# A mixed transformer kernel on one core: the second block's input projections as seven block products instead of eight, with the depthwise convolution cut into pieces between their sums

## The chip, the core and the metric

The kernel runs on one core of a Trainium2 chip. The metric is device microseconds (us) of one execution. Beside each run of a changed kernel the kernel before is run on the same chip. All data are float32; each matmul of the program appears in the trace as two instructions, each with its own weight load.

## The reference, cut to what matters

A first block (a mixer and a feed-forward part) hands a 512-token sequence of width 1024 to a second block of two layers. At the head of each layer a normalised input is projected to 2048 columns, and a depthwise convolution of 31 taps, followed by a layer norm and a SiLU, runs on 256 channels of the result:

```python
u = h @ w_in_l                                  # 1024 -> 2048 columns
q_a, k_a = apply_axial_rope(...), apply_axial_rope(...)   # 512 and 128 columns
v_a, q_b, k_b, v_b = ...                        # 128, 256, 256, 256 columns
o_c = conformer_conv(u[..., OFF_C:], ...)       # 2 x 256 columns

def conformer_conv(u, conv_w, conv_b, ln_g, ln_b):
    a, gate = jnp.split(u, 2, axis=-1)
    h = a * jax.nn.sigmoid(gate)
    h = lax.conv_general_dilated(h, conv_w, ...) + conv_b   # 31 taps, per channel
    return jax.nn.silu(layer_norm(h, ln_g, ln_b))
```

In the first layer 512 tokens and 256 context tokens are projected alike (768 in all). In the last layer the context tokens give only keys and values, so queries and convolution have 512 tokens. The outputs feed attention, an output projection and a mixture of 16 experts.

## The kernel before, in words

The program is a chain of blocks with a barrier after each; inside a block each engine runs its own list in the order in which it is written, and waits on semaphores. `project2` is the block of this case; it runs once for each layer. `uT` holds the input by channel (8 tiles of 128 channels, `KD`), and the 2048 columns of weights come in eight chunks of 256 columns (1 MB each) through `Stream`, a ring of eight slots in SBUF, which SyncE fills in the order of use: a chunk is asked for when the chunk before it in its slot has been freed, and no further than `stream.limit`. The tiles are named in the traces by their buffer: `ring` is the weight ring, `both` and `tokens_b` are the two large activation buffers (their roles swap between the layers), `ps` is PSUM.

TensorE works off `jobs`. A job is 128 output columns: eight matmuls (`KD`) for each of two halves of the tokens, 32 instructions in the trace. There are 15 such jobs; the values of the first attention (`va`) are made by tokens instead, as six jobs with 128-wide matmuls. Between the jobs stand five rotations (`rotate`, one matmul of 512 columns, for the rotary embedding) and three groups of transposes: `turn_z`, `turn_back` (the convolution's output to token order and back, around the layer norm) and `turn_values`. ScalarE empties each job from PSUM into its tile. VectorE waits for the first four jobs (`cin`, convolution input and gate), multiplies them into `pad`, runs the whole convolution (31 taps x 2 channel groups, L2743 and L2745), and after it the rotary products (`rope`), the layer norm's statistics (L2752 to L2761), the bias (L2771) and a copy (L2776). The next block, attention, starts when all are done.

The block `feed_up` of the first block (L2002 to L2160) already computes its products by the scheme that the change brings to `project2`, on halves of 257 tokens: seven products for eight, and sums on VectorE with a convolution of 3 taps behind them.

Of the kernel before, what the change touches and what calls it, by code (L numbers as in the profile page):

```python
# [727 lines left out]
def first_block(k):  # L728
    nc = k.nc
    stream, c1 = k.stream, k.c1  # L730
    with ExitStack() as outer:
        hT = k.hT
        with ExitStack() as ctx:
# [9 lines left out]
            k.stream.limit = len(k.stream.chunks)  # L743
# [1745 lines left out]
def layer(k, l, x, mod, a, b):  # L2489
# [7 lines left out]
    with ExitStack() as outer:  # L2497
        z = k.alloc(outer)("z", [P, 2, conv_width(nq)])
        with ExitStack() as inner:
# [20 lines left out]
            with ExitStack() as scope:  # L2520
                sbs = k.alloc(scope)
                tables = sbs("tables", [P, CONSTS[3][0].shape[1]])
                vt = sbs("vt", [P, 2, T2])
                k.at.update({n: (tables, v) for n, v in CONSTS[3][1].items()})
                k.stream.ahead = [(raw, k.dram["bias"][l]), (tables[:, :], k.dram["const3"])]
                raw = raw.rearrange("p (h c) -> p h c", h=NB)
                turned = [sbs("rtmp", [P, SEQ]), b[:, 4 * T2:4 * T2 + SEQ]]
                project2(k, sbs, mixT, nq, qa, ka, qb, kb, va, vb, cin, pad, z, zt, raw, bias, vt, turned)
# [42 lines left out]
def project2(k, sb, uT, nq, qa, ka, qb, kb, va, vb, cin, pad, z, zt, raw, bias, vt, tmp):  # L2571
# [4 lines left out]
    ready, taken, loads = k.sig["product"], k.sig["taken_s"], k.sig["load"]  # L2576
    rotated, rot_taken = k.sig["rotated"], k.sig["rot_taken"]
    filtered, z_turned, z_meant, z_rooted = k.sig["filtered"], k.sig["z_turned"], k.sig["z_meant"], k.sig["z_rooted"]
    z_normed, z_back, z_done = k.sig["z_normed"], k.sig["z_back"], k.sig["z_done"]
    NB, ntq = raw.shape[1], nq // P  # L2580
# [6 lines left out]
    jobs = [(chunk[i // 2], i % 2, cin[:, i // 2, i % 2, :], nq, "gate" if i // 2 else None) for i in range(4)]  # L2587
    jobs += [(chunk[2 + i // 2], i % 2, qa[:, i, :], nq, scale) for i in range(4)]
    jobs += [(chunk[4], 0, ka[:, :], T2, None)] + [(chunk[4], P, va[:, t, :], t, "tokens") for t in range(NT2)]
    jobs += [(chunk[5], j, qb[:, j, :], nq, "near_q") for j in range(2)]  # L2590
    jobs += [(chunk[6], j, vt[:, j, :], T2, "near") for j in range(2)]
    jobs += [(chunk[7], j, kb[:, j, :], T2, "near") for j in range(2)]
    KA, QB, VB, KB = 8, 9 + NT2, 11 + NT2, 13 + NT2
    turned = k.sig["v_turned"]
    lat = [qa[:, i, 0:SEQ] for i in range(4)] + [ka[:, 0:SEQ]]
    zp = psf[:, 4 * BANK:7 * BANK].rearrange("p (t c) -> p t c", c=2 * P)
    zq = psf[:, 4 * BANK:4 * BANK + 2 * nq].rearrange("p (g t) -> p g t", g=2)

    with nc.Block() as block:
        @block.tensor  # L2600
        def _(pe):
            def project(i):
                n, j, dst, size, kind = jobs[i]
                if i == 0 or jobs[i - 1][0] != n:
                    stream.wait(pe, n)
                if i >= 2:
                    pe.wait_ge(taken.sem, taken.of(i - 1))
                bank = 2 * (i % 2)
                if kind == "tokens":
                    s, width = stream.slot(n).rearrange("p (k c) -> p k c", k=KD), dst.shape[1]  # L2610
                    for c_ in range(KD):
                        mm = pe.matmul(ps[:, bank, 0:width], uT[:, c_, P * size:P * size + P], s[:, c_, j:j + width], start=c_ == 0,
                                       stop=c_ == KD - 1, skip_group_check=True)
                else:
                    w, half = column_chunk(k, n, j), size // 2
                    for c_ in range(KD):
                        for h in range(2):
                            mm = pe.matmul(ps[:, bank + h, 0:half], w(c_), uT[:, c_, h * half:(h + 1) * half], start=c_ == 0,  # L2618
                                           stop=c_ == KD - 1, skip_group_check=True)
                mm.then_inc(ready.sem, 1)  # L2620
                if i + 1 == len(jobs) or jobs[i + 1][0] != n:
                    stream.freed(n, ready.sem, ready.of(i + 1))

            def rotate(r):
# [4 lines left out]
                pe.wait_ge(taken.sem, taken.of(4 + r + 1))  # L2629
                pe.matmul(ps[:, 7, :], c("rot"), lat[r], start=True, stop=True).then_inc(rotated.sem, 1)  # L2630

            def turn_z():
                pe.wait_ge(filtered.sem, filtered.of(1))
                for t in range(ntq):
# [11 lines left out]
            def turn_values():  # L2646
                pe.wait_ge(taken.sem, taken.of(VB + 2))
                pe.wait_ge(z_done.sem, z_done.of(1))
                for t in range(NT2):
                    for j in range(2):  # L2650
                        at = 4 * BANK + t * 2 * P + j * P
                        mm = pe.transpose(psf[:, at:at + P], vt[:, j, P * t:P * t + P], c("ident"))
                mm.then_inc(turned.sem, 1)

            for i in range(len(jobs)):
                project(i)
                if i == KA:
                    rotate(0)
                elif i == QB:
                    rotate(1)  # L2660
                    turn_z()
                elif i == QB + 1:
                    rotate(2)
                elif i == VB:
                    turn_back()
                    rotate(3)
                elif i == VB + 1:
                    rotate(4)
                elif i == KB:
                    turn_values()  # L2670

        @block.scalar
        def _(act):
            steps = k.steps(act, "s")

            def evacuate(i):
                n, j, dst, size, kind = jobs[i]
                bank = 2 * (i % 2)
                act.wait_ge(ready.sem, ready.of(i + 1))
                if kind == "tokens":  # L2680
                    x = act.activation(dst, ps[:, bank, 0:dst.shape[1]], ACT.Identity)
                elif kind in ("near", "near_q"):
                    half = size // 2
                    parts = []
                    for h in range(2):
                        r0, n_rows = h * half // GRID_W, min(half, SEQ - h * half) // GRID_W
                        src = ps[:, bank + h, 0:n_rows * GRID_W]
                        parts += (near_queries if kind == "near_q" else near_keys_of)(dst[:, 0:SEQ], src, r0, r0 + n_rows)
                    if size > SEQ:
                        parts.append((dst[:, SEQ:size], ps[:, bank + 1, SEQ - half:half]))  # L2690
                    for out, src in parts[:-1]:
                        steps.free(act.activation(out, src, ACT.Identity, scale=scale if kind == "near_q" else 1.0))
                    steps.join()
                    x = act.activation(*parts[-1], ACT.Identity, scale=scale if kind == "near_q" else 1.0)
                else:
                    half = size // 2
                    out, src = dst[:, 0:size].rearrange("p (h t) -> p h t", h=2), ps[:, bank:bank + 2, 0:half]
                    if kind == "gate":
                        x = act.activation(out, src, ACT.Sigmoid)
                    else:  # L2700
                        x = act.activation(out, src, ACT.Identity, scale=1.0 if kind is None else kind)
                x.then_inc(taken.sem, 1)

            for i in range(len(jobs)):
                evacuate(i)
                if i == QB:
# [1082 lines left out]
```

## Time and profile before

| what | value |
|---|---|
| median of 3 runs | 2835.19 us (2834.72 to 2843.73) |
| the profiled execution: its own time | 2836.13 us |
| its span | 2834.3 us |
| TensorE busy | 2712.9 us, 96% |
| VectorE busy | 1091.4 us, 39% |
| ScalarE busy | 600.5 us, 21% |
| `project2`, first layer | 974.8 to 1152.0 us of the span |
| `project2`, last layer | 2004.0 to 2144.5 us of the span |

Times inside the profile are counted from the start of the span, which is 1.8 us shorter than the execution's own time. Matmuls are pipelined: the duration of one row overlaps the next, so the time that one costs is read from the distance between starts. A row of a timeline that merges instructions gives the start of the first and the time to the end of the last.

### The profile page before, as it was taken

The numbers are of one execution on the slowest core, as the hardware profiler recorded it, in microseconds if no ns is written. First come the engines' busy times: TensorE is split into PE (matmuls) and PEld (weight loads), VectorE is DVE, ScalarE is ACT, GpSimd is POOL, SyncE is SP. The second block draws the span as 40 slices with busy tenths as digits, with TensorE's granted clock in tenths as the row PEclk, the third lists the DMA queues.
The fourth block names the chain that finished last, engine by engine and source line by source line (L and its number), as shares of the span: only waits on it lengthen the run. The fifth ranks groups of instructions, "written<-read, shape, count | busy, mean of one in ns | idle before, by whom it ended". The sixth has DMA issues, their size and how long they took to land. (4 is left out here: it accounts for less than half of the span.)

```text
span 2834.3 us, 36392 instructions
## 1 busy us (share of the span) xinstructions
PE 2712.9 (96%) x15414; PEld 1568.9 (55%) x15414; DVE 1091.4 (39%) x2334; ACT 600.5 (21%) x1265; POOL 63.6 (2%) x61
## 2 busy tenths in 40 slices
PE   8998989999999999999799999999999989999998
PEld 7786755688864556764533333333777554444442
DVE  3523454477730365675620001113556560111212
ACT  4212234201110201562400000001215331001002
POOL 0000000000000000000001111110000000000000
PEclk9999999999999999999899999999999999999999
DMA  4228781222221211000489999996210038999995
GB/s 159 70 90 293 274 322 38 89 89 90 78 103 45 117 55 50 16 16 28 191 335 399 403 398 401 389 393 285 72 60 16 16 145 342 422 422 422 422 422 235
DMA packets 87478, 582.02 MB, mean 205 GB/s; under 512 B 10186, under 2 KB 11754, under 8 KB 21780
## 3 DMA queue, kind: packets, MB, share of 16 engines
q1 hardware_dynamic: 78244, 554.66, 49.3%
q0 software_dynamic: 6544, 21.24, 2.5%
q10 hardware_dynamic: 2528, 3.80, 0.4%
q8 instruction: 122, 2.00, 0.3%
q14 instruction: 40, 0.33, 0.0%
HBM read 561.96 MB, written 17.70 MB: 205 GB/s over the span
## 5 line engine op out<-in xcount | busy, mean ns | idle before, releaser
L3043 PE MATMUL ps<-ring,xsL 128*64 128x512 f32 x1320 | 298.2, 604 | 5.7 <-ACTq L217 5.7
L3043 PEld LDWEIGHTS ps<-ring,xsL 128*64 128x64 f32 x1320 | 96.2, 139 | 200.9 <-issue 194.9
L3301 DVE TENSOR_TENSOR hidL<-hidL,ps 128x1024 f32<-128x1024 f32 x16 | 19.5, 1221 | 473.6 <-PE ps L3043 473.6
L2618 PE MATMUL ps<-both,ring 128*128 128x384 f32 x480 | 158.0, 491 | 1.9 <-PEq L1834 1.9
L1841 PE MATMUL ps<-ring,actT 128*128 128x512 f32 x352 | 151.6, 592 | 1.1 <-PEq L2034 1.1
L3043 PE MATMUL ps<-ring,htL 128*64 128x512 f32 x640 | 143.9, 600 | 3.4 <-ACTq L217 3.2
L865 PE MATMUL ps<-both,ring 128*128 128x264 f32 x640 | 143.8, 386 | 1.4 <-PEq L642 1.4
L865 PEld LDWEIGHTS ps<-both,ring 128*128 128x128 f32 x640 | 121.4, 190 | 22.9 <-issue 2.3
L3331 ACT ACTIVATE hidL<-ps 128x1024 f32<-128x1024 f32 x16 | 16.4, 1024 | 541.7 <-PE ps L3051 303.4
L2618 PEld LDWEIGHTS ps<-both,ring 128*128 128x128 f32 x480 | 91.8, 192 | 66.5 <-issue 5.5
L2618 PE MATMUL ps<-tokens_b,ring 128*128 128x256 f32 (+1 forms) x480 | 121.9, 415 | 2.3 <-PEq L2223 2.3
L2039 PE MATMUL ps<-tsum,wsum 128*128 128x257 f32 x528 | 123.1, 382 | 0.0
L1841 PEld LDWEIGHTS ps<-ring,actT 128*128 128x128 f32 x352 | 66.6, 190 | 84.2 <-issue 84.2
L2039 PEld LDWEIGHTS ps<-tsum,wsum 128*128 128x128 f32 x528 | 101.2, 192 | 15.1
L2618 PEld LDWEIGHTS ps<-tokens_b,ring 128*128 128x128 f32 x480 | 90.9, 190 | 32.0 <-issue 3.9
L2745 DVE SCALAR_TENSOR_TENSOR z<-pad,both,z 128x783 f32<-128x783 f32 (+1 forms) x120 | 101.9, 890 | 2.1
L3043 PEld LDWEIGHTS ps<-ring,htL 128*64 128x64 f32 x640 | 45.3, 138 | 94.8 <-issue 93.8
L3051 PE MATMUL ps<-ring,xsC 128*32 128x512 f32 x768 | 88.8, 595 | 0.0
L2039 PE MATMUL ps<-both,ring 128*128 128x257 f32 x352 | 85.3, 386 | 1.6 <-PEq L1652 1.6
L595 ACT COPY probT<-ps 128x1024 f32<-128x1024 f32 (+4 forms) x80 | 74.3, 928 | 53.9 <-PE ps L488 53.6
L290 PE MATMUL ps<-const 128*128 128x256 f32 x342 | 81.6, 392 | 1.8 <-ACTq L217 1.7
L3043 PE MATMUL ps<-tokens_b,xsL 128*64 128x512 f32 x328 | 75.1, 595 | 0.0
(571 smaller groups left out, 3973.8 us busy)
## 6 DMA issues: line engine op xcount, KB each, us to landing
ring<-in_w_exp SPq DMA_DIRECT2D x245, 1024.0 KB, 13.7
ring<-in_w SPq DMA_DIRECT2D x73, 1024.0 KB, 5.0
tokens_b<-in_w_exp SPq DMA_DIRECT2D x63, 1024.0 KB, 13.8
ring<-in_w_mod SPq DMA_DIRECT2D x48, 1024.0 KB, 5.3
h<-in_w_exp SPq DMA_DIRECT2D x37, 1024.0 KB, 17.5
lent<-in_w_exp SPq DMA_DIRECT2D x26, 1024.0 KB, 15.9
both<-in_w_exp SPq DMA_DIRECT2D x13, 1024.0 KB, 18.6
gb<-in_rows SPq DMA_DIRECT2D x8, 512.0 KB
```

The costliest lines, as they stand in the source:

```text
L290: pe.matmul(k.ps[:, bank, 0:2 * P], table[:, 0:P], table[:, 0:2 * P], start=True, stop=True, skip_group_check=True)
L595: act.copy(probT[0:u["turn"], i % 2, 0:2 * nt, 0:u["n"]], T[0:u["turn"], 0:2 * nt, 0:u["n"]]).then_inc(pt_ready.sem, 1)
L865: mm = pe.matmul(ps[0:m, bank + h, 0:HALF1], lhs(c_), hT[:, c_, h * HALF1:(h + 1) * HALF1], start=c_ == 0, stop=c_ == KD - 1, skip_group_c ...
L1841: mm = pe.matmul(ps[:, 2 * j + half, :], actT[:, f, P * j:P * j + P], s[:, kk, half * BANK:(half + 1) * BANK], start=f == 0, stop=f == FT ...
L2039: mm = pe.matmul(out, w[:, c_, :], x[:, c_, :], start=start and c_ == 0, stop=c_ == K2 - 1, skip_group_check=True)
L2618: mm = pe.matmul(ps[:, bank + h, 0:half], w(c_), uT[:, c_, h * half:(h + 1) * half], start=c_ == 0, stop=c_ == KD - 1, skip_group_check=True)
L2745: steps.free(dve.scalar_tensor_tensor(z[:, g, :], src, w, z[:, g, :], ALU.mult, ALU.add))
L3043: mm = pe.matmul(ps[HD * par:HD * par + HD, bank + half, :], lhsL(kk, par), weights(kk)[:, half, par, :], start=kk == 0, stop=kk == KD - 1 ...
L3051: mm = pe.matmul(ps[q:q + CAP_C, cbank, :], lhsC(kk, par), weights(kk)[:, half, par, :], start=kk == 0, stop=kk == KD - 1, skip_group_chec ...
L3301: dve.tensor_tensor(h[:, :], h[:, :], src, ALU.mult).then_inc(hid.sem, 1)
L3331: act.activation(hidL[:, :], psf[:, GB * BANK:(GB + 2) * BANK], ACT.Silu).then_inc(silu.sem, 1)
```

## The change

For a chunk of 256 weight columns, the weights are split into 2 x 2 blocks (two halves of the input channels, two groups of 128 columns) and the tokens into two halves, `H` = 384 or 256. Instead of eight block products, seven are made (`P1 P7 P2 P6 P5 P4 P3` in the order of TensorE; each is four matmuls of `H` columns), and sums of blocks are formed on VectorE: four of the tokens (`t1` to `t4`, once), four of the weights for each chunk (`s1` to `s4`), and five of results for each chunk, which read PSUM. Both kinds of sums are held in four slots of the ring (`k.scratch`), so the eight weight chunks run through the other four, and `stream.limit` keeps output weights and experts out until the block has ended. `va` is now projected by channel too and turned by six transposes (`turn_va`). In the last layer, the context tokens of keys and values come from ordinary matmuls (`context`, 16 of 256 columns, three times). The convolution stays on VectorE, in nine pieces between the sums.

```diff
-            k.stream.limit = len(k.stream.chunks)
+            k.stream.limit = k.moe_at[0] - N_OUT2
...
+            stream.limit = k.moe_at[l + 1] - N_OUT2 if not last else len(stream.chunks)
...
-            for i in range(len(jobs)):
-                project(i)
+            for i in range(N_IN2):
+                stream.wait(pe, chunk[i])
+                if i:
+                    pe.wait_ge(copied.sem, copied.of(2 * i))
+                product(bank(0), block_of(i, 0, 0), b11)
+                if i == QB:
+                    turn_va()
+                elif i == KB:
+                    rotate(3)
+                pe.wait_ge(weight_sums.sem, weight_sums.of(3 * i + 1))
+                if i:
+                    pe.wait_ge(assembled.sem, assembled.of(4 * i - 1))
+                product(bank(1), s3, t3)
+                pe.wait_ge(copied.sem, copied.of(2 * i + 1))
+                product(bank(0), block_of(i, 0, 1), b21, start=False)
+                if i == VB:
+                    turn_z()
+                pe.wait_ge(weight_sums.sem, weight_sums.of(3 * i + 2))
...
+                product(bank(2), s2, t2)
...
+                product(bank(3), s1, t1)
+                if i == VB:
+                    turn_back()
+                pe.wait_ge(weight_sums.sem, weight_sums.of(3 * i + 3))
+                pe.wait_ge(assembled.sem, assembled.of(4 * i + 1))
+                product(bank(1), block_of(i, 1, 1), t4)
+                if i == QB:
+                    rotate(1)
+                pe.wait_ge(assembled.sem, assembled.of(4 * i + 2))
+                product(bank(3), s4, b22, start=False)
+                if i in kv:
+                    context(i)
...
+            def first_sums(i):
...
+                dve.wait_ge(ready.sem, ready.of(at(i, P6)))
+                steps(plus(part(i, 0, 1), bank(2), part(i, 0, 0)))
+                steps.free(plus(part(i, 1, 0), bank(1), part(i, 0, 1)))
+                steps.tell(assembled.sem)
...
+            def second_sum(i):
...
+                dve.wait_ge(ready.sem, ready.of(at(i, P5)))
+                steps.free(plus(part(i, 1, 1), bank(3), part(i, 1, 0)))
+                steps.tell(assembled.sem)
+                if i + 1 < N_IN2:
+                    stream.wait(dve, chunk[i + 1])
+                    steps.free(minus(s3, block_of(i + 1, 0, 0), block_of(i + 1, 1, 0)))
+                    steps.free(plus(s1, block_of(i + 1, 1, 0), block_of(i + 1, 1, 1)))
+                    steps.tell(weight_sums.sem)
...
+            convolve(0, 3)
+            first_sums(QA)
...
+            last_sum(KA)
+            convolve(15, 23)
+            first_sums(QB)
+            second_sum(QB)
+            rope(0)
+            third_sum(QB)
+            last_sum(QB)
+            convolve(23, CW)
             dve.sem_inc(filtered.sem, 1)
-            rope(0)
             rope(1)
             dve.wait_ge(z_turned.sem, z_turned.of(1))
...
+            first_sums(KB)
+            second_sum(KB)
             dve.wait_ge(z_done.sem, z_done.of(1))
+            add_bias(0, 2)
+            third_sum(KB)
+            rope(4)
+            add_bias(2, len(NEAR_PIECES))
+            last_sum(KB)
```

`third_sum` and `last_sum` wait for P4 and P3 in the same way, make one sum of results, and then one of the weights of the next chunk.

VectorE's order at the head of the first layer's `project2` before, where `z` is the convolution's output: one run of 62 convolution instructions, with the rotary products behind it.

```order
L2730 MEMSET pad 128x1626
L2733 TENSOR_TENSOR pad<-tokens_b 128x2x512
L2736 TENSOR_TENSOR pad<-tokens_b 128x2x256
L2743 TENSOR_SCALAR z<-pad,both 128x783 x2
L2745 SCALAR_TENSOR_TENSOR z<-pad,both,z 128x783 x60
L2725 TENSOR_TENSOR rtmp<-ps,tables 128x512
```

The same engine in the change, from the sixteenth tap of the convolution to its end (the chunk between is `QB`; `ring` as an output is a weight sum for the chunk behind it).

```order
L2846 SCALAR_TENSOR_TENSOR z<-pad,both,z 128x783 x16
L2796 TENSOR_TENSOR tokens_b<-ps,tokens_b 128x384 x3
L2799 TENSOR_TENSOR ring<-ring 128x512
L2796 TENSOR_TENSOR ring<-ring 128x512
L2851 TENSOR_TENSOR rtmp<-ps,tables 128x512
L2852 TENSOR_TENSOR qa<-qa,tables 128x512
L2854 TENSOR_TENSOR qa<-qa,rtmp 128x512
L2799 TENSOR_TENSOR tokens_b<-tokens_b,ps 128x384
L2799 TENSOR_TENSOR ring<-ring 128x512
L2796 TENSOR_TENSOR tokens_b<-ps,tokens_b 128x384
L2799 TENSOR_TENSOR ring<-ring 128x512
L2846 SCALAR_TENSOR_TENSOR z<-pad,both,z 128x783 x16
```

The results of `QB` and the weight sums for `VB` now stand between two pieces of eight taps; before, no product of TensorE waited for VectorE here.

TensorE in the first layer in the change, from `turn_va` in chunk `QB` (L2662) to `turn_back` in chunk `VB` (L2677); L2634 is the products, L2655 a rotation, L2670 `turn_z`.

```order
L2662 MATMUL ps<-const,tokens_b 128x128 x6
L2634 MATMUL ps<-ring 128x384 x4
L2634 MATMUL ps<-both,ring 128x384 x4
L2634 MATMUL ps<-ring 128x384 x12
L2655 MATMUL ps<-qa,tables 128x512
L2634 MATMUL ps<-both,ring 128x384 x8
L2634 MATMUL ps<-ring 128x384 x4
L2634 MATMUL ps<-both,ring 128x384 x4
L2670 MATMUL ps<-const,z 128x128 x12
L2634 MATMUL ps<-ring 128x384 x4
L2655 MATMUL ps<-qa,tables 128x512
L2634 MATMUL ps<-ring 128x384 x4
```

Before, the first job of `qb` stood ahead of `turn_z`: six jobs of 32 instructions and the six jobs of `va` lay between the last input of the convolution and it. Now four chunks (`QA`, `QA2`, `KA`, `QB`) and three products of `VB` do.

## Rows read from the trace of the kernel before

**Rows 1.** Busy time by stretch; the columns are named in the first row.
```profile
core 0: us, PE busy (x) PEld busy (x) DVE busy (x) ACT busy (x) POOL busy (x), PEclk, DMA share, GB/s
974.80:1152.00 177.20, 175.91 (x622) 108.47 (x622) 84.48 (x109) 22.15 (x49) 0.00 (x0) 0.99 0.17 66
1152.00:1300.00 148.00, 143.29 (x1167) 97.05 (x1168) 108.24 (x378) 84.69 (x186) 0.00 (x0) 0.99 0.04 15
...
2004.00:2144.00 140.00, 138.98 (x614) 106.65 (x614) 64.47 (x102) 18.46 (x44) 0.00 (x0) 1.00 0.19 67
```
**Rows 2.** Timeline of TensorE, first layer: start, us, what, idle before.
```profile
974.85 95.04 PE L2618 MATMUL ps<-both,ring 128*128 128x384 f32 x288 [1.93 <-PEq L1834]
...
1070.59 10.88 PE L2612 MATMUL ps<-ring,both 128*128 128x128 f32 x96
1081.30 10.49 PE L2618 MATMUL ps<-both,ring 128*128 128x384 f32 x32
1091.63 1.02 PE L2630 MATMUL ps<-qa,tables 128*128 128x512 f32 x2
1092.48 1.47 PE L2636 MATMUL ps<-const,z 128*128 128x128 f32 x12
...
1140.27 10.49 PE L2618 MATMUL ps<-both,ring 128*128 128x384 f32 x32
```
**Rows 3.** Timeline of TensorE, last layer.
```profile
2081.55 7.07 PE L2618 MATMUL ps<-tokens_b,ring 128*128 128x256 f32 x32
2088.46 1.02 PE L2630 MATMUL ps<-qa,tables 128*128 128x512 f32 x2
...
2132.82 10.49 PE L2618 MATMUL ps<-tokens_b,ring 128*128 128x384 f32 x32
```
**Rows 4.** Timeline of VectorE, first layer.
```profile
1021.04 1.28 DVE L2743 TENSOR_SCALAR z<-pad,both 128x783 f32<-128x783 f32 x2
1022.36 60.44 DVE L2745 SCALAR_TENSOR_TENSOR z<-pad,both,z 128x783 f32<-128x783 f32 x60
1082.95 0.69 DVE L2725 TENSOR_TENSOR rtmp<-ps,tables 128x512 f32<-128x512 f32 x1
...
1094.73 2.08 DVE L2752 BATCH_NORM_STATS2 stats<-ps 128x6 f32<-128x256 f32 x6
...
1098.06 2.80 DVE L2761 TENSOR_SCALAR tokens_b<-ps,mv,rstd 128x256 f32<-128x256 f32 x6
...
1130.89 3.16 DVE L2771 TENSOR_TENSOR tokens_b<-tables,tokens_b 128x512 f32<-128x512 f32 x6
```
**Rows 5.** Timeline of VectorE, last layer.
```profile
2035.16 43.47 DVE L2745 SCALAR_TENSOR_TENSOR z<-pad,both,z 128x512 f32<-128x512 f32 x60
```
**Rows 6.** Timeline of VectorE in `feed_up`, its start and its first chunk.
```profile
532.60 1.23 DVE L2087 TENSOR_TENSOR tsum<-both 128x1028 f32<-128x1028 f32 x1 [0.84 <-PEq L1652]
...
542.76 0.89 DVE L2084 TENSOR_TENSOR part<-ps,part 128x257 f32<-128x257 f32 x2 [2.51 <-PE ps L2039]
544.50 0.42 DVE L2084 TENSOR_TENSOR raw<-ps,part 128x257 f32<-128x257 f32 x1 [0.85 <-PE ps L2039]
545.07 0.69 DVE L2087 TENSOR_TENSOR wsum<-ring 128x512 f32<-128x512 f32 x1
...
546.51 0.42 DVE L2087 TENSOR_TENSOR raw<-part,ps 128x257 f32<-128x257 f32 x1
```
**Rows 7.** Timeline of TensorE in `feed_up`, the P4 of that chunk.
```profile
544.22 1.90 PE L2039 MATMUL ps<-tsum,ring 128*128 128x257 f32 x8
```
**Rows 8.** Timeline of ScalarE, end of the first layer's `project2`.
```profile
1151.61 0.38 ACT L2694 ACTIVATE kb<-ps 128x256 f32<-128x256 f32 x1
```
**Rows 9.** Busy time by stretch after two idle times of TensorE (columns as in rows 1).
```profile
974.85:978.65 3.80, 3.80 (x6) 2.15 (x7) 1.41 (x1) 0.00 (x0) 0.00 (x0) 0.50 1.03 433
...
2354.00:2355.00 1.00, 1.00 (x6) 0.28 (x4) 0.00 (x0) 0.00 (x0) 0.00 (x0) 0.85 0.95 401
```
**Rows 10.** Timeline of TensorE, the second of those idle times.
```profile
2348.47 7.82 PE L3043 MATMUL ps<-ring,xsL 128*64 128x512 f32 x22 [3.04 <-ACTq L217]
```

More of the change, by code:

```diff
@@ L2601, in _, with product, context @@
         def _(pe):
[L2602 to L2610, printed above, removed]
-                    for c_ in range(KD):
[L2612 to L2619, printed above, removed]
+            def product(out, w, x, start=True):
+                for c_ in range(K2):
+                    mm = pe.matmul(out, w[:, c_, :], x[:, c_, :], start=start and c_ == 0, stop=c_ == K2 - 1, skip_group_check=True)
+                mm.then_inc(ready.sem, 1)
+            def context(i):
+                for j in range(2):
+                    w = column_chunk(k, chunk[i], j)
+                    for c_ in range(KD):
+                        mm = pe.matmul(ps[:, 2, j * CTX:(j + 1) * CTX], w(c_), uT[:, c_, SEQ:T2], start=c_ == 0, stop=c_ == KD - 1,
+                                       skip_group_check=True)
                 mm.then_inc(ready.sem, 1)
-                if i + 1 == len(jobs) or jobs[i + 1][0] != n:
-                    stream.freed(n, ready.sem, ready.of(i + 1))
             def rotate(r):
@@ L2674, in _ @@
             steps = k.steps(act, "s")
[L2676 to L2699, printed above, removed]
-                    else:
-                        x = act.activation(out, src, ACT.Identity, scale=1.0 if kind is None else kind)
-                x.then_inc(taken.sem, 1)
@@ new lines, in convolve @@
+            def convolve(first, after):
+                for tap in range(first, after):
+                    for g in range(2):
+                        w, src = c2("conv_w", 2 * tap + g), pad[:, g, tap:tap + n_out]
+                        if tap == 0:
+                            steps.free(dve.tensor_scalar(z[:, g, :], src, w, c2("conv_b", g), ALU.mult, ALU.add))
+                        else:
+                            steps.free(dve.scalar_tensor_tensor(z[:, g, :], src, w, z[:, g, :], ALU.mult, ALU.add))
+                    steps.join()
@@ L2733, in _ @@
+            steps.free(minus(s4, block_of(0, 0, 1), s2))
+            steps.tell(weight_sums.sem)
+            steps.free(dve.memset(pad[:, :, :], 0.0))
+            for i in (CIN, GATE):
+                first_sums(i)
+                second_sum(i)
+                third_sum(i)
+                last_sum(i)
+            dve.wait_ge(finished.sem, finished.of(1))
             steps.free(dve.tensor_tensor(pad[:, :, CH_HALF:CH_HALF + SEQ], cin[:, 0, :, 0:SEQ], cin[:, 1, :, 0:SEQ], ALU.mult))
             if nq > SEQ:
-                at = CONV_CTX + CH_HALF
@@ L2781, in _ @@
             stream.issue(sp)
-    ready.close(len(jobs))
-    taken.close(len(jobs))
+    ready.close(7 * N_IN2 + len(kv))
+    copied.close(2 * N_IN2)
+    assembled.close(4 * N_IN2)
+    weight_sums.close(3 * N_IN2)
+    finished.close(6)
+    ctx_read.close(len(kv))
     loads.close(32)
```

234 lines of the change are left out of this document (171 added, 63 removed).

## The prediction

> **What bounds the kernel now.** The kernel is a chain of blocks, so I look at `project2` alone. The busy times by stretch come first: TensorE works 175.9 of 177.2 us in the first layer's block and 139.0 of 140.0 in the last layer's, VectorE 84.5 and 64.5 [rows 1]. TensorE bounds both blocks, and matmuls taken away shorten them only if nothing else ends last instead. Then the timelines give prices. On TensorE a job of 32 instructions of 384 columns takes 1091.63 - 1081.30 = 10.33 us (10.32 in the others), one of 256 columns 2088.46 - 2081.55 = 6.91, the six jobs of `va` 1081.30 - 1070.59 = 10.71, a rotation 1092.48 - 1091.63 = 0.85 [rows 2, 3]. The reader should see in VectorE's timeline that the convolution is one run: 1.32 us for the first tap and 60.44 for thirty, so 2.015 a tap, 1.45 in the last layer; that it ended at 1082.8, 9.7 us before `turn_z` at 1092.5; and that VectorE was behind nobody [rows 2, 4, 5].
>
> **What is taken away.** A product is a quarter of a job: 2.58 us at 384 columns, 1.73 at 256. First layer: 15 x 10.32 + 10.71 = 165.5 before, 56 x 2.58 = 144.5 after, and `turn_va` adds 6 transposes, by the twelve of `turn_z` at about 0.11 each 0.7. TensorE saves 20.4. Last layer: ten jobs of 256 columns, five of 384 and `va`, 69.1 + 51.6 + 10.7 = 131.4; after, 56 x 1.73 = 96.7, three `context` of 6.91 = 20.7 and 0.7. It saves 13.3. Together 33.7 us.
>
> **What VectorE gets.** `feed_up` has the same sums. Two dependent sums of 257 columns took 0.89 us, one 0.42; from P5's result to the first weight sum 545.07 - 544.50 = 0.57; VectorE starts 0.28 us after the product's modelled end (544.22 to 544.50) [rows 6, 7]. Estimated from 0.42 for 257 columns and 0.69 for 512 (the slope is 0.00105 us a column), a sum of 384 columns takes 0.56. So, with the waits between, `first_sums` costs 1.25 us, `second_sum` with two weight sums 2.1, `third_sum` and `last_sum` 1.45 each: 6.25 a chunk, and 5.7 in the last layer (1.0, 1.97, 1.36, 1.36). A `rope` is 2.1 (three such instructions). That is no matter of load: 8 x 6.25 = 50 us more in the first layer, 135 of 177. It is a matter of order. Each chunk's P4 needs `first_sums` of its own chunk, which VectorE can start only when its piece of convolution is over, and `turn_z` needs the last tap.
>
> **The first layer step by step**, from the end of `GATE`'s P3 as zero. A chunk takes TensorE 7 x 2.58 = 18.06 us. `last_sum`, the sigmoid and the two products into `pad` end at 3.8, three taps at 9.2; P6 of `QA` ends at 10.3, so nothing waits. From `QA`'s `last_sum` (19.8) five taps (10.1) reach 29.9, `first_sums` 31.15, while P5 of `QA2` ends at 30.96: 0.25 us lost, and 0.3 in the same place of `KA`. Behind `KA` stand eight taps: 56.55 + 16.1 = 72.65, `first_sums` 73.9. TensorE has finished P5 of `QB`, with a rotation and `turn_va`, at 69.2: it waits 4.75 us. P4 then runs late, `rope(0)` ends at 78.1, P3 at 81.9, `last_sum` at 83.6 and the last eight taps at 99.75. TensorE has done three products of `VB` at 89.7 and waits for `turn_z` 10.2 us. Behind it the norm takes what it took: statistics to the last product 1100.86 - 1094.73 = 6.1 us [rows 4], beside P6, a rotation and P5 (6.0), so `turn_back` loses next to nothing, and no later product waits. TensorE ends at 136.6. At the end VectorE has the bias (3.16 us, [rows 4]), `rope(4)` and two sums beside P4 and P3 (5.2 us), so `last_sum` ends some 3.1 us after TensorE, and ScalarE's rearrangement of the last tile behind it: 4.2 us from the last matmul to the barrier. Before, it was 1151.99 - 1150.76 = 1.2 [rows 2, 8]: 3.0 lost. In the first chunk, the sums of the tokens (1028 columns take 1.23 us, [rows 6], so 1.76 for 1536) hide behind the first three products.
>
> **The clock.** After 1.93 us of idle time that followed sparse work, the granted clock was 0.50 for 3.8 us, and after 3.04 us of idle time it came back at about 2354.3, 5.8 us after the work did [rows 2, 9, 10]. A drop to 1.2 GHz costs half of that, 1.9 to 2.9 us. The waits of 4.75 and 10.2 us will each bring one; I take 1.9 twice, by the row of this very block. The page "TensorE: Matmul & The Clock Gate" of the Trainium skill (section "Why this matters for your kernels") advises against idle gaps between bursts of matmuls for this reason; on that page's rule the change, which puts gaps where there were none, speaks against itself, and the trace agrees that short gaps cost more than their length.
>
> **Sum, first layer:** -20.4 + 0.55 (small waits) + 4.75 + 10.2 + 3.8 (clock) + 3.0 (end) = +1.9 us.
>
> **The last layer** goes the same way with 12.1 us a chunk. At the start the token sums do not quite hide (P7, P6 and, behind the memset of `pad`, P4: 1.4 us). Five taps are 7.25 us against 5.6 between `last_sum` and the next P6: `QA2` loses 1.3, `KA` 2.3. `context` (6.9 us) covers the first eight taps, so `QB`'s P4 does not wait, but the rotation behind it waits 2.0 for `rope(0)`. The last taps end at 76.6, TensorE is ready at 68.5: 8.2 for `turn_z`, and 1.9 of clock. The end is covered by `context`. Sum: -13.3 + 1.4 + 3.6 + 2.0 + 8.2 + 1.9 = +3.8; my steps, with rounding, gave +3.3.
>
> **Outside the block.** SyncE asks for eight in-chunks ahead before and four after; a chunk lasts 12 us or more and four are always ahead, so no product should wait for weights. The four output chunks and four expert chunks, loaded during `project2` before, move to the head of attention: 8 MB at the 433 GB/s of [rows 9] are 19 us in a block of 148 us in which the transfers' share is 0.04 [rows 1]. I cost this at nothing; without that cover it would be those 19 us twice.
>
> **Total:** 1.9 + 3.3 = +5.2 us. The sum is made in one execution of 2836.13 us; the median of the runs is 0.9 lower, and I set it on the median: 2840.4 us. Bounds of the uncertain terms: hand-overs between engines (some 30 on the path, each 0.1 either way, 3 us), the clock 0 to 2.9 us for each of up to five gaps (-5.7 to +9), a sum reading PSUM from 0.42 (the 257-column row) to 0.69 (the 512-column row), which moves the vector chain by -3 to +3 us over both layers.
>
> **Rivals.** *Savings kept, faster.* If VectorE's chain from `GATE` to the last tap is shorter than I count, `turn_z` is reached by TensorE's own work and the change keeps most of the 33.7 us. The chain is 31 taps (62 us), four chunks of sums (25), a `rope` and the start (6), 93 us and some 6 of idle time, against 82 of TensorE: the taps are measured, so 17 us would have to be wrong. My waits and ends sum to 38.9; the kernel is faster by more than 0.3% only if they stay below 25.2. With the waits halved, 14 us less than the forecast: 2822. Chance 0.12. *The clock, slower.* Every gap over 2 us (`KA`, twice at `QB`, twice at `turn_z`) costs 2.9, and P4 of `QB` at half speed pushes P3, `last_sum` and the last taps: 14.5 for my 5.7, so 2849. It decides from 3.3 us above the forecast, since slower means above 2843.7. For it speaks the second row of the clock, against it that gaps near 2 us behind dense work have no such row. Chance 0.27. *The moved transfers.* If the output or expert weights come late or hold up attention by a quarter of the 38 us: 2850; nothing in the trace speaks for it. Chance 0.03.
>
> **How the numbers follow.** What a measurement can tell from no change is about 0.3%, 8.5 us: 2826.7 to 2843.7. My forecast, that the waits eat the saving and the time stays inside, has 0.58; its own range is 2832 to 2843.7. Faster 0.12, slower 0.27 + 0.03 = 0.30. The range for 8 in 10 takes in the slower cases but for their end, and the upper half of the faster: 2827 to 2851.
>
> **What would show it.** TensorE's timeline of the first layer should have an idle time of 4 to 5 us before `QB`'s P4 and of about 10 before `turn_z`, both released by VectorE, and a last-layer one of about 8; PEclk near 0.5 behind them; `project2` about 179 and 143.5 us long against 177.2 and 140.2; attention and experts unchanged to a microsecond. If TensorE's busy time falls by less than 30 us after correction for the clock, the unit prices are wrong. The forecast fails if the sums on VectorE overlap the convolution better than their starts in `feed_up` say, or if TensorE waits at places where I found none (P2 for ScalarE's copies, P7 for weight sums).

## The result: 0.45% slower, and the profile after

The changed kernel took 2847.86 us (median of 9 runs) against 2835.64 for the kernel before: a ratio of 1.0045, 95% interval 1.0034 to 1.0057, so 12.8 us (9.6 to 16.2) where 5.2 was forecast. It lies inside the range of the prediction (2827 to 2851) but above 2843.7, where its likeliest case ended; it came out where the rival "the clock, slower" had put it (2849). Two executions, one of `late_even_filled` (5605 us) and one of the kernel before (4032 us), ran in a much slower state and count in no number below.

The timeline of TensorE in the first layer of the changed kernel (start, us, what, idle before) answers to [rows 2]:

```profile
971.16 5.46 PE L2634 MATMUL ps<-both,ring 128*128 128x384 f32 x8 [2.32 <-PEq L1834]
976.41 3.03 PE L2634 MATMUL ps<-ring 128*128 128x384 f32 x8
979.27 2.74 PE L2634 MATMUL ps<-both,ring 128*128 128x384 f32 x8
...
1074.66 5.32 PE L2634 MATMUL ps<-ring 128*128 128x384 f32 x16
1084.76 5.22 PE L2634 MATMUL ps<-ring 128*128 128x384 f32 x8 [4.78 <-DVEq L217]
1089.82 1.02 PE L2655 MATMUL ps<-qa,tables 128*128 128x512 f32 x2
...
1111.20 2.82 PE L2670 MATMUL ps<-const,z 128*128 128x128 f32 x12 [10.04 <-DVEq L2916]
1113.81 4.29 PE L2634 MATMUL ps<-ring 128*128 128x384 f32 x8
...
1121.38 1.47 PE L2677 MATMUL ps<-const,tokens_b 128*128 128x128 f32 x12
...
1146.36 2.74 PE L2634 MATMUL ps<-both,ring 128*128 128x384 f32 x8
1153.39 1.15 PE L476 MATMUL ps<-ka,qa 64*128 64x128 f32 x12 [4.29 <-PEq L2629]
```

The two waits stand where they were forecast, and with their lengths: 4.78 us before P4 of `QB` (forecast 4.75), 10.04 before `turn_z` (10.2), both until VectorE. The end of the block took 4.3 us from TensorE's last product to the first of attention. What was not forecast is the length of what follows a wait: P4 took 1089.82 - 1084.76 = 5.06 us instead of 2.58, and from `turn_z` to `turn_back` went 10.18 us, for 7.33 us of work (1.31 + 2.58 + 0.86 + 2.58).

VectorE in the same stretch (answers to [rows 4]) works without idle time through the piece of eight taps that holds P4 up, and through the one that holds `turn_z` up:

```profile
1067.27 16.09 DVE L2846 SCALAR_TENSOR_TENSOR z<-pad,both,z 128x783 f32<-128x783 f32 x16
1083.40 1.85 DVE L2796 TENSOR_TENSOR tokens_b<-ps,tokens_b 128x384 f32<-128x384 f32 x3
...
1095.00 16.09 DVE L2846 SCALAR_TENSOR_TENSOR z<-pad,both,z 128x783 f32<-128x783 f32 x16
```

TensorE in the last layer (answers to [rows 3]):

```profile
2057.93 1.97 PE L2634 MATMUL ps<-ring 128*128 128x256 f32 x8 [1.15 <-DVEq L217]
...
2072.48 3.59 PE L2634 MATMUL ps<-ring 128*128 128x256 f32 x8 [2.00 <-DVEq L217]
2075.87 1.99 PE L2634 MATMUL ps<-tokens_b,ring 128*128 128x256 f32 x8
...
2098.37 1.12 PE L2655 MATMUL ps<-qa,tables 128*128 128x512 f32 x2 [1.73 <-DVEq L2853]
...
2114.35 1.97 PE L2670 MATMUL ps<-const,z 128*128 128x128 f32 x8 [7.95 <-DVEq L2916]
...
2122.57 1.04 PE L2677 MATMUL ps<-const,both 128*128 128x128 f32 x8
```

1.15, 2.00, 1.73 and 7.95 us stand where 1.3, 2.3, 2.0 and 8.2 were forecast. In these rows a granted clock of 0.5 is the half clock, 1.2 of 2.4 GHz. The clock behind four of the waits, in the stretch from each resumption to the next thing on TensorE that is not late (columns as in [rows 1]):

```profile
1084.76:1089.82 5.06, 5.06 (x9) 2.81 (x10) 3.77 (x6) 0.36 (x1) 0.00 (x0) 0.52 0.00 0
1111.20:1121.38 10.18, 10.18 (x31) 6.72 (x31) 8.67 (x25) 0.21 (x1) 0.00 (x0) 0.72 0.00 0
2072.48:2075.87 3.39, 3.39 (x8) 2.68 (x9) 3.08 (x5) 0.26 (x1) 0.00 (x0) 0.53 0.00 0
2114.35:2122.57 8.22, 8.22 (x27) 6.49 (x27) 6.79 (x19) 0.58 (x2) 0.00 (x0) 0.63 0.00 0
```

A share c of the clock over a stretch costs (1 - c) of it: 2.4, 2.9, 1.6 and 3.0 us. TensorE's own busy time hides this, since slow products count as busy.

### The profile page after: what moved, and what is told of

Its sections match the earlier page's. It is cut to its first block and busy times, and to the rows that moved or that the text cites. A ratio compares the mean times of both kernels' runs of the same rounds, so it can differ in the third digit from the quotient of the medians.

```text
span 2846.0 us, 36446 instructions
## 1 busy us (share of the span) xinstructions
PE 2695.0 (95%) x15266; PEld 1563.4 (55%) x15266; DVE 1180.8 (41%) x2480; ACT 609.9 (21%) x1269; POOL 63.5 (2%) x61
## 5 line engine op out<-in xcount | busy, mean ns | idle before, releaser
L2634 PE MATMUL ps<-ring 128*128 128x384 f32 (+1 forms) x512 | 154.0, 453 | 8.3 <-DVEq L217 8.2
L865 PEld LDWEIGHTS ps<-both,ring 128*128 128x128 f32 x640 | 121.4, 190 | 23.2 <-issue 2.6
L2634 PEld LDWEIGHTS ps<-ring 128*128 128x128 f32 x512 | 101.5, 201 | 54.3 <-issue 17.2
L290 PEld LDWEIGHTS ps<-const 128*128 128x128 f32 x342 | 67.2, 200 | 16.4 <-issue 4.0
L2039 PEld LDWEIGHTS ps<-both,ring 128*128 128x128 f32 x352 | 67.7, 193 | 11.6 <-issue 1.8
```

The source lines that it names most:

```text
L290: pe.matmul(k.ps[:, bank, 0:2 * P], table[:, 0:P], table[:, 0:2 * P], start=True, stop=True, skip_group_check=True)
L865: mm = pe.matmul(ps[0:m, bank + h, 0:HALF1], lhs(c_), hT[:, c_, h * HALF1:(h + 1) * HALF1], start=c_ == 0, stop=c_ == KD - 1, skip_group_c ...
L2039: mm = pe.matmul(out, w[:, c_, :], x[:, c_, :], start=start and c_ == 0, stop=c_ == K2 - 1, skip_group_check=True)
L2634: mm = pe.matmul(out, w[:, c_, :], x[:, c_, :], start=start and c_ == 0, stop=c_ == K2 - 1, skip_group_check=True)
```

## The experiments

The length of each part of the program in the profiles, from the first product of `project2` to the first of attention (first layer), from there to the last layer's `project2` ("between"), that block, and what lies ahead of all this ("head"), in us; "time" is the median of the runs, and the ratio compares them with runs of the kernel before taken beside them (it is not the quotient of two medians; for `early_gap` that would be 1.0089):

| kernel | head | first layer | between | last layer | time | ratio (95%) |
|---|---|---|---|---|---|---|
| before | 974.85 | 177.45 | 852.03 | 140.52 | 2835.64 | |
| before_again | 982.05 | 177.41 | 852.02 | 140.53 | | |
| the change | 971.16 | 182.23 | 856.57 | 147.26 | 2847.86 | 1.0045 (1.0034 to 1.0057) |
| change_again | 972.31 | 182.36 | 856.55 | 147.27 | 2849.83 | 1.0034 (1.0016 to 1.0052) |
| short_filter | 971.72 | 164.06 | 857.44 | 136.56 | 2818.47 | 0.9940 (0.9919 to 0.9961) |
| filled_waits | 985.48 | 178.25 | 850.52 | 145.89 | 2845.61 | 1.0026 (1.0012 to 1.0040) |
| cut_at_20 | 974.91 | 180.84 | 854.96 | 145.24 | 2848.51 | 1.0044 (1.0028 to 1.0059) |
| transfers_only | 978.54 | 177.01 | 851.95 | 140.52 | 2838.95 | 1.0008 (0.9991 to 1.0024) |
| late_turn | 975.52 | 175.04 | 857.33 | 141.58 | 2840.38 | 1.0003 (0.9991 to 1.0015) |
| late_even | 978.74 | 171.51 | 853.57 | 139.26 | 2830.08 | 0.9979 (0.9964 to 0.9994) |
| late_even_filled | 974.33 | 170.49 | 853.51 | 140.50 | 2830.96 | 0.9961 (0.9943 to 0.9979) |
| early_gap | 972.33 | 193.74 | 855.05 | 151.22 | 2864.65 | 1.0102 (1.0074 to 1.0131) |

The code of the head and of "between" is the same in all (but for what SyncE asks for). The start of a block is no fixed cost either: the first two products of the changed first layer took 8.11 us in the change, 7.20 in `filled_waits` and 7.22 in `cut_at_20`, those of the last layer 5.22, 6.51 and 3.77, with the clock as the difference. Lengths of blocks are compared below with that in mind.

**short_filter** takes the load away that makes VectorE late; it leaves out sixteen of the 31 taps.

```diff
-            convolve(15, 23)
             first_sums(QB)
...
-            convolve(23, CW)
```

> Leaves out taps 15 to 30 of the convolution in both layers (the two pieces of eight taps), so VectorE has 32 us less to do in the first layer and 23 in the last. Theory 'order on VectorE': TensorE then waits neither for P4 of QB (4.8 us in the changed kernel's trace) nor at turn_z (10.0 and 8.0), nor pays the half clock behind these waits (2.5, 2.9 and 3.0 us lost in its rows); about 1 us comes back as a wait of the rotation for rope(0). 30 us less than the changed kernel: 2817 to 2819 us, clearly faster than the kernel before. Rival 'the block products themselves cost more than counted' (prices of products, PSUM reads, transfers): the time falls by less than half of that, to 2833 or more, and the stretches between the waits in project2 are longer than 18.06 and 12.1 us a chunk.

Measured 2818.47 us, inside what the first theory gave. The waits of 4.78, 10.04 and 7.95 us are gone, and the two blocks have shrunk by 18.2 and 10.7 us; their clock is back:

```profile
971.72:1135.78 164.06, 157.77 (x501) 92.25 (x501) 101.30 (x150) 27.56 (x51) 0.00 (x0) 0.98 0.11 38
1993.22:2129.78 136.56, 129.53 (x588) 109.26 (x589) 82.64 (x143) 23.66 (x49) 0.00 (x0) 0.99 0.13 46
```

So the seven products cost what was counted, and the saving is real; in the first layer it was mainly the convolution between the sums that took it. The block is now 13.4 us shorter than before there, of the 20.4 saved on TensorE. In the last layer it is only 4.0 shorter, of 13.3: the waits of 1.15, 2.00 and 1.7 us are still there, with 1.8 us of half clock behind the second, since none of them hangs on the taps left out.

**cut_at_20** asks whether each wait counts by itself, or one chain of VectorE ends them all.

```diff
-            convolve(15, 23)
+            cut = 20 if nq > SEQ else 23
+            convolve(15, cut)
...
-            convolve(23, CW)
+            convolve(cut, CW)
```

> The changed kernel with the two pieces of eight taps cut as five and eleven in the first layer (the last layer as it is). Theory 'one chain on VectorE up to the last tap': the wait of 4.8 us before P4 of QB goes, and the wait at turn_z grows from 10.0 to about 15 or 16; turn_z starts within 1 us of where it was, and the time stays within 1.5 us of the changed kernel (2846 to 2849). Rival 'each wait adds its own length': the time falls by the 4.8 us and the 2.5 us of clock behind it, to about 2840.

```profile
1113.97 2.82 PE L2670 MATMUL ps<-const,z 128*128 128x128 f32 x12 [16.11 <-DVEq L2917]
```

The wait at `QB` is gone, the one at `turn_z` has grown from 10.04 to 16.11 us, and `turn_z` starts 139.06 us into the block, for 140.04 in the change, of which 0.9 comes from the clock at the block's start. The time is the changed kernel's (ratio 1.0044). The chain it is: where the pieces are cut moves the wait, not the end.

The last layer's code is unchanged here, yet its block is 2.0 us shorter than in the change (145.24 for 147.26). The rows of its start and of P4 of `KA`:

```profile
2010.71 1.97 PE L2634 MATMUL ps<-tokens_b,ring 128*128 128x256 f32 x8 [2.28 <-PEq L2223]
...
2020.66 1.97 PE L2634 MATMUL ps<-ring 128*128 128x256 f32 x8 [0.45 <-DVEq L217]
2022.46 3.62 PE L2634 MATMUL ps<-tokens_b,ring 128*128 128x256 f32 x16
...
2072.86 1.96 PE L2634 MATMUL ps<-ring 128*128 128x256 f32 x8 [2.00 <-DVEq L217]
2074.79 1.99 PE L2634 MATMUL ps<-tokens_b,ring 128*128 128x256 f32 x8
```

The same wait of 2.00 us stands before P4 of `KA`, but the product behind it ran at full clock, 1.93 us for the change's 3.39. At the start the clock was full too, and TensorE then waited for the sums of the tokens: it came to P3 after 11.75 us for 12.12, so the half clock of the change's start cost only 0.4 us there.

**filled_waits** keeps TensorE busy where it waits.

```diff
+                if i == QB and nq > SEQ:
+                    keep_busy(k, pe, 6, 9)
+                elif i == KA and nq == SEQ:
+                    keep_busy(k, pe, 6, 3)
                 pe.wait_ge(assembled.sem, assembled.of(4 * i + 1))
...
+                    keep_busy(k, pe, 6, 21 if nq > SEQ else 17)
                     turn_z()
```

> The changed kernel with idle matmuls (256 columns, into an unused bank) put where TensorE waits: 9 before P4 of QB in the first layer, 3 before P4 of KA in the last, 21 and 17 before turn_z; they take about 0.43 us each, no longer than the waits. Theory 'the clock was undercounted': P4, turn_z and the products behind them run at full speed; P4 of QB ends 2.5 us sooner of which the rotation gives back 0.9, turn_back starts 1.8 us sooner in the first layer and 1.5 in the last, P4 of KA 1.7: 6 to 7 us less than the changed kernel, about 2841 us. Rival 'only the waits count and the half clock hides beside them': no change within 1.5 us, 2847 to 2849.

```profile
1098.08 2.85 PE L2634 MATMUL ps<-ring 128*128 128x384 f32 x8 [0.80 <-DVEq L217]
1101.66 1.12 PE L2655 MATMUL ps<-qa,tables 128*128 128x512 f32 x2 [0.73 <-DVEq L2858]
...
1123.16 1.53 PE L2670 MATMUL ps<-const,z 128*128 128x128 f32 x12 [0.99 <-DVEq L2921]
...
1131.49 1.53 PE L2677 MATMUL ps<-const,tokens_b 128*128 128x128 f32 x12 [0.78 <-DVEq L217]
```

P4 now takes 2.85 us in its row for 5.22 in the change, and `turn_back` starts 8.33 us behind `turn_z` instead of 10.18, the 1.8 us expected. The blocks are 4.0 and 1.4 us shorter. Their first two products, which the edit does not touch, took 0.9 us less and 1.3 more than in the change; without that the gain is 3.1 and 2.7 us, 5.7 of the 6 to 7. The median fell by only 2.3 us, to 2845.61, between the two theories; by the times of the runs they stay unseparated here (the intervals of the ratios overlap), and it is the profile that speaks for the first.

**transfers_only** is the kernel before with the stream's part of the change alone (`stream.limit`, and four slots of the ring withheld during `project2`, which nothing uses).

> The kernel before with only the stream's part of the change: input weights run through four slots, output weights and experts are asked for from attention on; all computation is as before. Theory 'transfers are hidden': the same time as before, within 1 us (2835 to 2836.5). Rival 'the moved transfers cost': the changed kernel's profile has 4.5 us more between the two project2 blocks than before's, 3.1 of it in the experts; if that is theirs, 2839 to 2840.

```profile
978.54:1155.55 177.01, 175.47 (x622) 108.31 (x623) 84.49 (x109) 22.18 (x50) 0.00 (x0) 0.99 0.10 35
1155.55:2007.50 851.95, 819.70 (x5038) 357.58 (x5039) 282.12 (x755) 193.81 (x429) 63.38 (x57) 0.98 0.70 274
2007.50:2148.02 140.52, 138.98 (x614) 106.65 (x615) 64.47 (x102) 19.01 (x46) 0.00 (x0) 1.00 0.13 44
```

All three parts are as before to 0.5 us, "between" too. The median, 2838.95, is above what the first theory gave and near the rival's 2839; its interval holds no change and the rival's 4.5 us alike, so the runs decide nothing. The profile does: its head is 3.7 us longer, which the edit does not touch, and the part in which the rival's 4.5 us should stand is 851.95 us for 852.03. The transfers are hidden.

**change_again and before_again**, for the 4.5 us that the profile of the change had between the blocks.

> The changed kernel once more, for a second profile. If the 4.5 us more between its two project2 blocks and the 3.7 us less ahead of the first one are chance of the clock, they come out otherwise here (before has 852.0 us between and 974.9 ahead), while the lengths of the two project2 blocks stay within 2 us of 182.2 and 147.3. If they belong to the change, they come back.

> The kernel before once more, for a second profile: the lengths of its two project2 blocks within 1 us of 177.5 and 140.5, the stretches outside them free to differ by some us, if they are chance.

```profile
972.31:1154.67 182.36, 162.87 (x500) 95.48 (x501) 133.08 (x182) 27.53 (x51) 0.00 (x0) 0.93 0.10 34
1154.67:2011.22 856.55, 824.52 (x5038) 359.60 (x5039) 282.19 (x755) 193.66 (x429) 63.30 (x57) 0.97 0.70 273
2011.22:2158.49 147.27, 133.22 (x588) 112.76 (x589) 105.30 (x175) 23.65 (x49) 0.00 (x0) 0.94 0.12 42
```

```profile
982.05:1159.46 177.41, 175.87 (x622) 108.47 (x623) 84.51 (x109) 22.18 (x50) 0.00 (x0) 0.99 0.18 65
1159.46:2011.48 852.02, 819.78 (x5038) 358.19 (x5039) 282.08 (x755) 193.84 (x429) 63.29 (x57) 0.98 0.69 271
2011.48:2152.01 140.53, 138.98 (x615) 106.66 (x615) 64.49 (x103) 19.01 (x46) 0.00 (x0) 1.00 0.19 68
```

Both come back to within 0.15 us. The 4.5 us between are the change's (852.02 against 856.55), the 3.7 us ahead were chance: the kernel before has 974.85 and 982.05 there. The rows name the cause of the first: 0.97 for 0.98 of the clock. Summed over windows of 10 us, (1 - granted clock) times the length is 22.1 us between the blocks of the change and 15.4 before. (That sum counts idle time at half clock too, so it is more than the 4.5 us by which the part grew.) It goes with the length over the kernels of the table: 12.2 in `filled_waits`, which has the shortest "between", 15.4 in `transfers_only`, 23.2 and 23.3 in `late_turn` and `short_filter`, which have the longest. The first ten microseconds of attention are one place: 0.83 in the change, 1.00 before. In all seven kernels where TensorE idles 3.6 or 4.3 us at the end of the first layer's block it is 0.69 to 0.84 there, in the three where it idles 1.5 us it is 1.00. That is 1.7 us of the 4.5, and it is not the whole matter: `filled_waits` pays it and has the shortest "between" of all. The other differences lie where both kernels have short idle times of about the same length, ahead of the last layer's block for one, and only one of them is slowed.

**early_gap** measures the disputed price by itself, in the kernel before, where no other code moves.

```diff
+                if i == KA + 1:
+                    pe.wait_ge(filtered.sem, filtered.of(1))
                 bank = 2 * (i % 2)
```

> The kernel before, but TensorE waits for the last tap of the convolution ahead of the first job of va instead of at turn_z, where it came too late to matter. Nothing else moves, so this is a pure wait of about 12.2 us in the first layer and 7.9 us in the last, in front of 128-column matmuls. Theory 'a wait costs its length and 2.5 to 3 us of half clock': project2 grows by 12.2 + 2.5 to 3 and 7.9 + 2.5 to 3 us, the kernel by 25 to 26 us to about 2861. Rival 'the length and 1.9' (what the prediction used): 23.9. Rival 'the length only': 20.1.

```profile
972.33 96.00 PE L2620 MATMUL ps<-both,ring 128*128 128x384 f32 x288 [2.33 <-PEq L1834]
...
1081.46 13.77 PE L2614 MATMUL ps<-ring,both 128*128 128x128 f32 x96 [12.27 <-DVEq L2749]
1095.07 10.49 PE L2620 MATMUL ps<-both,ring 128*128 128x384 f32 x32
```

```profile
2095.61 13.59 PE L2614 MATMUL ps<-ring,tokens_b 128*128 128x128 f32 x96 [7.83 <-DVEq L2749]
2109.04 7.07 PE L2620 MATMUL ps<-tokens_b,ring 128*128 128x256 f32 x32
```

The six jobs of `va` take 1095.07 - 1081.46 = 13.61 and 13.43 us for 10.71 before [rows 2]: 2.9 and 2.7 us for a drop behind these two waits. The blocks grew by 16.3 and 10.7 us; 1.0 of the 16.3 is the clock at the block's start (96.00 us for 95.04 in [rows 2]), which no wait of this edit precedes. The kernel grew by 25.2 us by the medians and by 21 to 37 by the interval, which holds all but the lowest rival, so it is the rows that decide: in these two places a drop cost more than 1.9.

**late_turn, late_even and late_even_filled** put the finding to use: the last tap comes late, so put the work that doesn't need it in front of `turn_z`.

```diff
                 if i == VB:
-                    turn_back()
+                    turn_z()
+                elif i == KB:
+                    turn_values()
...
-            rope(0)
             third_sum(QB)
             last_sum(QB)
             convolve(23, CW)
             dve.sem_inc(filtered.sem, 1)
-            rope(1)
+            first_sums(VB)
+            second_sum(VB)
+            rope(0)
+            third_sum(VB)
             dve.wait_ge(z_turned.sem, z_turned.of(1))
```

`turn_back` moves behind P7 of `KB`, the rotations behind it. `late_even` cuts the convolution as its expectation says (in nine pieces in both layers), and the third adds `keep_busy` before `turn_z`.

> The changed kernel with what hangs on the last tap put later: turn_z behind P5 of VB instead of behind P2, turn_back behind P7 of KB, rope(0) taken out of VectorE's chain and put behind the last tap, first and second sums of VB ahead of the statistics. Pieces of convolution as in the change. Theory 'the last tap is late, and TensorE has work left to put in front of it': the wait at turn_z falls from 10.0 to about 5 us in the first layer and from 8.0 to about 3 in the last, the rotation's wait at QB goes, the wait of 4.8 before P4 of QB stays; 10 us less than the changed kernel, 2836 to 2839. Rival 'the norm behind turn_z is the path (statistics, root, turn back, SiLU, values), and moving it back moves the end of the block': the end of the block is reached no sooner, and the time stays at 2845 or more.

> late_turn with the 31 taps in ten pieces of 3, 1, 5, 1, 5, 1, 5, 1 and 9 (first layer; nine pieces) and 3, 1, 4, 1, 4, 1, 7, 1, 9 (last layer), a single tap standing between the first and the second sum of each chunk. Theory: no chunk's P4 waits for a piece (the 4.8, 1.2 and 2.0 us go with the half clock behind them), VectorE's idle times in the chain shrink, and the last tap ends 5 us sooner in the first layer and 3 in the last: 2827 to 2831, faster than the kernel before by 5 to 8 us. Rival 'the chain is what it is, only the place of the wait moves': turn_z starts where it did in late_turn, and the time is late_turn's within 2 us.

> late_even with 14 and 6 idle matmuls of 256 columns before turn_z. If the half clock behind a wait of 8 and 6 us costs what it cost in the changed kernel (2.9 and 3.0 us between turn_z and P5), 3 to 5 us less than late_even: 2823 to 2827. If it hides beside VectorE's statistics: the same as late_even within 1.5 us.

`late_turn` took the two blocks from 182.2 and 147.3 to 175.0 and 141.6 us; 2840.38 us is 1.4 above what I gave it, and the norm is not the path. `late_even` left no wait for P4 above 0.54 us and landed in its range: 0.9979 of the kernel before. `turn_z` came 3.2 and 1.3 us sooner into its block than in `late_turn`, for 5 and 3 expected. In the last layer it waited 6.77 us, and the stretch behind it took 4.35 us for 2.60 of work:

```profile
2104.08 1.97 PE L2670 MATMUL ps<-const,z 128*128 128x128 f32 x8 [6.77 <-DVEq L2920]
2105.84 2.75 PE L2634 MATMUL ps<-ring 128*128 128x256 f32 x8
2108.43 1.89 PE L2634 MATMUL ps<-tokens_b,ring 128*128 128x256 f32 x8
```

So a drop can also cost 1.75 us. Over the changed kernels and `early_gap` there are thirteen waits for VectorE of some 4.2 us and more; behind each the clock fell, and the work behind it took 1.7 to 3.0 us longer, 2.5 in the mean. What sets a single one is open: waits of 4.78 us (the change) and 4.77 (`late_turn`) before the same P4 cost 2.5 and 1.8.

Filling the waits brought nothing that the medians show (2830.96 for 2830.08). In the first layer `turn_z` then ran at full speed, but `turn_back` waited 1.84 us for VectorE's statistics: what the half clock had cost hides beside them, and the block gained 1.0 us. In the last layer six idle matmuls were too few; a wait of 4.17 us was left and the clock fell behind it, and the 1.2 us by which the block is longer were lost in its first two products. The ratio is nevertheless the best, 0.9961, with an interval that overlaps `late_even`'s. Its blocks:

```profile
974.33:1144.82 170.49, 163.85 (x529) 97.63 (x529) 132.88 (x183) 27.33 (x51) 0.00 (x0) 0.98 0.10 36
...
1998.33:2138.83 140.50, 134.03 (x600) 113.96 (x601) 105.28 (x175) 23.54 (x49) 0.00 (x0) 0.97 0.12 44
```

Both versions beat the kernel before and the change. What they gain is mostly the first layer's 6 to 7 us; the last layer is still nearly as long as with plain jobs (139.26 and 140.50 us for 140.52), since its saving of 13.3 us meets a wait of 6.8 at `turn_z`, the clock behind it and at the block's start, and small waits.

## Why the prediction was right in its steps and short in its sum

- *Prices of products and sums.* Right. A product took 2.58 us, the two sums of `first_sums`, with the hand-over to P4, 1.36 for 1.25 (1083.40 to 1084.76); a sum of 384 columns 0.56 as interpolated. short_filter confirms the saving. TensorE's busy time fell by 17.9 us, and with the clock's 12.8 and 4.5 (below) given back by 35, over the 30 that the prediction set as its sign.
- *The order on VectorE.* Right: all six waits of TensorE are within 0.3 us of the forecast, and cut_at_20 shows the single chain.
- *The end of the first layer's block.* Right in length, 4.3 us of idle time for 4.2. That attention would start at half clock behind it was not counted.
- *"The clock": "I take 1.9 twice, by the row of this very block", and once in the last layer, 5.7 in all.* This term was too small. Six stretches of the two blocks ran at half clock for all or part of their length: 2.95 us lost at the start of the first layer (P1 and P7 took 8.11 us for 5.16; before, 2.0), 2.5 behind `QB`'s wait, 2.85 behind `turn_z`; 1.8 at the start of the last, 1.7 at `KA` behind a wait of only 2.00 us, 3.0 behind `turn_z`. That is 14.8, less 2.0 that was there before: 12.8 for 5.7. The lengths are off by less: the first layer +4.8 for +1.9, the last +6.7 for +3.3. The rest of the sum explains that. In the first layer the clock is 2.5 us over its term (6.3 for 3.8), in the last 4.6 (6.5 for 1.9), but there it stands in the place of the 1.4 us for the sums of the tokens, which stayed hidden behind the slow start, and the last layer's waits were 1.0 us shorter than forecast. Small losses of 0.1 to 0.4 us at several places, about 1 in each layer by difference, were hardly counted. In number, the drop at `KA` and what the clock took at the two block starts were missing; in price, the 2.9 us that the prediction had read from [rows 9, 10] was nearer than 1.9 to what the waits at `QB` and `turn_z` cost (2.5, 2.85, 3.0; 2.9 and 2.7 in early_gap), though drops of 1.8 came too.
- *"Outside the block ... I cost this at nothing."* Right for the transfers, by transfers_only; wrong for the stretch, and so is the sign "attention and experts unchanged to a microsecond". 4.5 us came there with the clock. The forecast had no term for it, nor had the rival. In attention's first microseconds (1.7 us) the low clock goes with the longer idle time at the barrier in every kernel; for the places further on, it is shown only that they come back in a second profile of the change and that the clock makes them, not why just those.
- *The sum.* 4.8 + 4.5 + 6.7 = 16.0 us by the profiles, 12.8 (9.6 to 16.2) by the runs; 5.2 forecast. The rival "the clock, slower" had the mechanism, and deserved more than 0.27. I had its price in my own rows and chose the lower one because it stood in the same block. That its time comes out so well is in part luck: it has 14.0 us in the two blocks, where 11.5 were measured, and none of the 4.5 between them.
- *Slips in the sums.* The printed terms of the last layer add up to +3.8, and the forecast used +3.3; with +3.8 it would have been 2840.9. In the rival "Savings kept, faster", 14 us less than the forecast is 2826.4 and not 2822. Neither moves the range.
- The page "TensorE: Matmul & The Clock Gate" of the Trainium skill (section "Why this matters for your kernels") warns of idle gaps between bursts of matmuls from a certain length on. The trace agrees in kind, and is stricter than the page in part: a wait of 2.00 us, shorter than the page's limit, was followed by the half clock in the change, `short_filter` and `late_turn`, and by the full clock in `cut_at_20`. No half clock followed the waits of 1.15 us.

## What to carry to other kernels

Taking a share of the matmuls away pays only if the sums that replace them find VectorE free at the moment when TensorE needs them: with 133 us of work in 182, order decided, not load: `late_turn` and `late_even` have the same sums and taps, and are 7.5 and 17.8 us faster than the change by the medians. When another engine's long chain must end before a step of TensorE, write down TensorE's work that does not hang on it and put that in front; where the chain is cut moves only the place of the wait. And count each new wait of TensorE of some 4 us or more at its length plus 1.7 to 3 us of half clock, at the ends of blocks too; a wait of 2 us may or may not bring a drop, here 1.7 to 1.8 us in three kernels and nothing in a fourth.

## What the runs showed that was not expected

The two kernels that were profiled twice agree with themselves to 0.2 us in every part behind the head, drops of the clock included (before: 177.45 and 177.41, 852.03 and 852.02, 140.52 and 140.53). But "between", with the same code, runs from 850.52 to 857.44 us over ten different kernels, by where the clock falls; a change can gain or lose 4 us in code that it does not touch. The head, which is the same code in all, varies from execution to execution even of one kernel. The rows of the place where its two profiles of the kernel before differ most (before, then before_again) show the half clock once more:

```profile
380.00:400.00 20.00, 16.07 (x205) 10.51 (x198) 8.30 (x19) 2.85 (x7) 0.00 (x0) 1.00 0.94 356
```

```profile
380.00:400.00 20.00, 18.64 (x189) 11.66 (x187) 4.00 (x15) 2.37 (x6) 0.00 (x0) 0.59 0.70 255
```

That is 8.2 us lost in 20, enough for the 7.2 us by which the two heads differ. These two executions took 2836.13 and 2842.96 us, so the head makes all of their difference; whether it makes most of the scatter of the runs (2830 to 2848 us for the kernel before), two profiles cannot show. The scatter of the head is why parts of a profile separate theories here that medians do not. Why the clock falls there in some runs stays open.
